# Gate products and convolution taps placed between the heads of the first attention

## What is computed

```python
h = rmsnorm(x, norm1_g)
z = h @ w_in + b_in
glu_val, glu_gate, q, k, v, g_conv, g_attn = split(z)
u = glu_val * sigmoid(glu_gate)                        # 1024 channels
y = depthwise_causal_conv(u, 31 taps) + conv_b
conv_out = silu(layernorm(y) * ln_g + ln_b) @ w_conv_out
q, k = rope(q), rope(k)                                # 16 query heads, 2 key heads
attn_out = sink_attention(q, k, v, window=128) @ w_attn_o
merged = sigmoid(g_conv) * conv_out + sigmoid(g_attn) * attn_out
x = x + merged @ w_out
```

## Time and profile before

| what | value |
|---|---|
| median of 3 runs | 1798.57 us |
| profiled execution, its own time | 1801.52 us |
| its span on the core | 1799.5 us |
| PE busy | 84% |
| DVE, ACT busy | 54%, 32% |
| granted clock of TensorE, mean | 0.95 |
| first layer up to the start of `wout` | 303.16 us of the span |

### The profile page before, as it was taken

How to read it: one execution, slowest core, us unless ns; L and a number is a source line. 1 busy time by engine, 2 the same in 40 slices (tenths; PEclk the granted TensorE clock), 3 DMA queues, 4 the chain that set the end, 5 groups by cost and what they waited for, 6 DMA issues and landing times.

```text
span 1799.5 us, 18415 instructions
## 1 busy us (share of the span) xinstructions
...
## 2 busy tenths in 40 slices
...
GB/s 256 198 214 152 1 47 141 126 408 386 389 421 420 419 420 416 411 420 419 408 409 420 398 48 173 53 94 140 130 179 176 177 111 153 63 125 188 188 187 47
DMA packets 52023, 428.69 MB, mean 238 GB/s; under 512 B 6880, under 2 KB 7032, under 8 KB 9824
## 3 DMA queue, kind: packets, MB, share of 16 engines
...
## 4 chain that ended last, share of the span: by engine, by line
PE 63%; DMA 19%; DVE 10%; ACT 5%; issue 2%; POOL 0%; DVEq 0%; SPq 0%; ACTq 0%; POOLq 0%
PE psum L595 21%; DMA pool<-uv,experts 17%; PE psum L813 10%; PE psum L686 9%; PE psum L687 9%; PE psum L688 9%; DVE pool L1473 3%; PE psum L628 2%; PE psum L644 2%; DMA ring<-stream 1%; DVE w_lo L1263 1%; ACT L1097 1%; ACT diag L1107 1%; ACT xn L904 1%; DVE hT L1198 1%
## 5 line engine op out<-in xcount | busy, mean ns | idle before, releaser
L813 PE MATMUL psum<-pool,diag 128*128 128x512 f32 x1024 | 489.1, 628 | 151.7 <-ACT diag L1107 141.9
L813 PEld LDWEIGHTS psum<-pool,diag 128*128 128x128 f32 x1024 | 195.4, 199 | 441.3 <-ACT diag L1107 223.0
L1473 DVE CUSTOM_DVE_ANT_0 pool<-pool,xn 128x1024 f32<-128x1024 f32 x256 | 313.8, 1226 | 216.5 <-DMA pool<-uv,experts 215.2
L552 POOL DMA_INDIRECT pool<-uv,experts x256 | 273.6, 1069 | 714.7 <-PE psum L813 371.7
L1263 DVE TENSOR_TENSOR w_lo<-ring,w_hi 128x2048 fp32r<-128x2048 f32 x86 | 196.8, 2292 | 218.2 <-ACT w_hi L961 218.2
L961 ACT ACTIVATE w_hi<-ring 128x2048 fp32r<-128x2048 f32 x86 | 164.3, 1914 | 326.4 <-PE psum L688 326.4
L686 PE MATMUL psum<-h_hi,w_hi 128*128 128x256 f32 x704 | 201.6, 286 | 22.4 <-DVE h_lo L1274 22.4
L687 PE MATMUL psum<-h_lo,w_hi 128*128 128x256 f32 x704 | 201.1, 286 | 0.0
L688 PE MATMUL psum<-h_hi,w_lo 128*128 128x256 f32 x704 | 201.1, 286 | 0.0
L595 PE MATMUL psum<-hT,ring 128*128 128x256 f32 x768 | 171.2, 385 | 5.4 <-DMA ring<-stream 2.8
L595 PEld LDWEIGHTS psum<-hT,ring 128*128 128x128 f32 x768 | 148.2, 193 | 28.8 <-issue 5.1
...
## 6 DMA issues: line engine op xcount, KB each, us to landing
...
pool<-uv,experts POOLq DMA_INDIRECT x256, 12.6
...
```

What stands on the lines that cost most here:

```text
L552: gp.indirect_dma_start(out=gath[:, n % NROWS, :], out_offset=None, in_=uv, in_offset=bass.IndirectOffsetOnAxis(ap=experts[:, n:n + 1], ax ...
L813: last = nc.tensor.matmul(psum[:, RB + half, :], diag[:, n % NDIAG, :], gath[:, n % NROWS, D + 512 * half:D + 512 * half + 512], start=k = ...
L1473: ins = V.tensor_tensor_reduce(out=row_u, in0=row_u, in1=xn[:, n // SLOTS, :], scale=1.0, scalar=0.0, op0=ALU.mult, op1=ALU.add, accum_out ...
```

## The change

- The gate products are made tile by tile (`GATES`, 16 of them). Six run before q and k are transposed, one after that, eight between heads of attention (after heads 0, 1, 3, 5, 7, 9, 11 and 13) and the last behind the first transposes of the attention's output. ACT no longer takes their sigmoid but copies them raw; two blocks of eight sigmoids come later (`gate_sigmoids`).
- The taps are counted through by `conv_taps(n)`: 27, 27, 27 and 67 behind the four GLU results, then the rotation, then 7 in each head of attention, 3 behind the mask and 4 behind the maximum, until all 248 are done (14 heads with 7, one with 2, one with none).
- q and k are rotated behind tap 148 instead of tap 186 (and no longer wait for the two stores, whose sources move out of `att`, to `pool` and `tab`).
- The layer norm moves behind attention: `mean` stands between the two pairs of output transposes, `var` behind the first quarter of `attno`; `attno` comes before `convout`, also in the stream of weights.
- The merge of the two branches is made in four pieces, each behind a quarter of `convout`, and `wout` waits for a piece at a time.

The diff, without the moved scratch tables, the new semaphore, the functions that only gather the transposes of the output, and the removed lines of `conv_pair`:

```diff
@@ -77,7 +77,7 @@
...
-    out += [(("convout", i), 4096) for i in range(2)] + [(("attno", i), 4096) for i in range(2)]
+    out += [(("attno", i), 4096) for i in range(2)] + [(("convout", i), 4096) for i in range(2)]
@@ -98,6 +98,27 @@
...
+GATES = [("gate", n // 4, n % 4) for n in range(16)]
+GATES_FIRST = 6
+GATE_AFTER_HEAD = {0: 7, 1: 8, 3: 9, 5: 10, 7: 11, 9: 12, 11: 13, 13: 14}
+GATE_LAST = 15
+CONV_TAPS = KD * TAPS
+TAPS_AFTER_GLU = (27, 27, 27, 67)
+TAPS_IN_HEAD = 7
+def att1_fills():
+    out = [("att1", "S", 0), ("att1", "S", 1)]
+    for h in range(QH):
+        out.append(("att1", "T", h))
+        if h + 2 < QH:
+            out.append(("att1", "S", h + 2))
+        if h in GATE_AFTER_HEAD:
+            out.append(GATES[GATE_AFTER_HEAD[h]])
+    out += [("att1", "OT", 0, t) for t in range(NT)] + [GATES[GATE_LAST], ("mean",)]
+    return out + [("att1", "OT", 1, t) for t in range(NT)]
@@ -130,10 +151,11 @@
...
-    out += fm_fills("gate", 4)
-    out += [("q1T", t, half) for t in range(NT) for half in range(2)] + [("k1T",), ("mean",), ("var",)]
-    out += attention_fills("att1", QH)
-    out += fm_fills("convout", 2) + fm_fills("attno", 2) + tm_fills("wout", 2)
+    out += GATES[:GATES_FIRST]
+    out += [("q1T", t, half) for t in range(NT) for half in range(2)] + [("k1T",), GATES[GATES_FIRST]]
+    out += att1_fills()
+    out += [("attno", 0, 0), ("var",), ("attno", 0, 1), ("attno", 1, 0), ("attno", 1, 1)]
+    out += fm_fills("convout", 2) + tm_fills("wout", 2)
@@ -158,6 +180,8 @@
...
+for i in range(4):
+    LAST_USE["gate", i] = ("gate", i, 3)
@@ -637,7 +663,21 @@
...
-            def attention(a):
+            def gate(n):
+                name, i, m = GATES[n]
+                w = wait_chunk(pe, (name, i))[:, 0:4096].rearrange("p (k n) -> p k n", k=KD)
+                dst = begin(GATES[n])
+                accumulate(dst[:, 0:S], [(w[:, k, P * m:P * m + P], hT[:, k, :]) for k in range(KD)]
+                           ).then_inc(bank_filled, 1)
+            def attention(a, gate_after={}):
@@ -669,12 +709,11 @@
...
+                    if h in gate_after:
+                        gate(gate_after[h])
...
+                if a.heads == HEADS2:
+                    turn_outputs(a, 0)
@@ -751,31 +790,54 @@
...
-            feature_major("gate", 4)
+            for n in range(GATES_FIRST):
+                gate(n)
...
-            pe.wait_ge(conv_ready, 4)
-            accumulate(begin(("mean",))[:, 0:S], [(ones, y[:, k, :]) for k in range(KD)]).then_inc(bank_filled, 1)
-            pe.wait_ge(ysq_ready, 1)
-            accumulate(begin(("var",))[:, 0:S], [(ones, ysq[:, k, :]) for k in range(KD)]).then_inc(bank_filled, 1)
+            gate(GATES_FIRST)
...
-            attention(att1)
+            attention(att1, GATE_AFTER_HEAD)
+            turn_outputs(att1, 0)
+            gate(GATE_LAST)
+            pe.wait_ge(conv_ready, 4)
+            accumulate(begin(("mean",))[:, 0:S], [(ones, y[:, k, :]) for k in range(KD)]).then_inc(bank_filled, 1)
+            turn_outputs(att1, 1)
+            wait_turned(att1)
+            def feature_major_pair(name, i, pair, act):
+                w = wait_chunk(pe, (name, i))[:, 0:4096].rearrange("p (k n) -> p k n", k=KD)
+                dst = begin((name, i, pair))
+                for j in range(2):
+                    c = P * (2 * pair + j)
+                    last = accumulate(dst[:, S * j:S * j + S], [(w[:, k, c:c + P], act[:, k, :]) for k in range(KD)])
+                last.then_inc(bank_filled, 1)
+            feature_major_pair("attno", 0, 0, oT)
+            pe.wait_ge(ysq_ready, 1)
+            accumulate(begin(("var",))[:, 0:S], [(ones, ysq[:, k, :]) for k in range(KD)]).then_inc(bank_filled, 1)
+            feature_major_pair("attno", 0, 1, oT)
+            feature_major_pair("attno", 1, 0, oT)
+            feature_major_pair("attno", 1, 1, oT)
...
-            wait_turned(att1)
-            feature_major("attno", 2, oT)
-            pe.wait_ge(merged_ready, 1)
-            token_major_chunks("wout", 2, hT)
+            for i in range(2):
+                w = wait_chunk(pe, ("wout", i))[:, 0:4096].rearrange("p (k n) -> p k n", k=KD)
+                for t in range(NT):
+                    dst = begin(("wout", i, t))
+                    for k in range(KD):
+                        if k % 2 == 0 and i == 0 and t == 0:
+                            pe.wait_ge(merged_ready, k // 2 + 1)
+                        last = nc.tensor.matmul(dst, hT[:, k, tile128(t)], w[:, k, :], start=(k == 0), stop=(k == KD - 1))
+                    last.then_inc(bank_filled, 1)
@@ -918,7 +980,27 @@
...
-            def attention(a):
+            def gate_copy(n):
+                m = n % KD
+                if n == KD:
+                    act.wait_ge(rpb_stored, 16 * RPB_ROWS)
+                empty(GATES[n], (sgc if n < KD else sga)[:, m, :], lambda b: b[:, 0:S])
+            def gate_sigmoids(g, first):
+                for n in range(first, first + KD):
+                    wait_emptied(act, GATES[n])
+                    nc.scalar.activation(g[:, n % KD, :], g[:, n % KD, :], ACT.Sigmoid, bias=par_("b_gate")[:, n:n + 1]
+                                         ).then_inc(gate_ready, 1)
+            def attention(a, gate_after={}):
@@ -1039,15 +1120,8 @@
...
-            for i in range(4):
-                for pair in range(2):
-                    b = wait_filled(act, ("gate", i, pair))
-                    for j in range(2):
-                        m = 4 * i + 2 * pair + j
-                        dst = (sgc if m < KD else sga)[:, m % KD, :]
-                        last = nc.scalar.activation(dst, b[:, S * j:S * j + S], ACT.Sigmoid,
-                                                    bias=par_("b_gate")[:, m:m + 1])
-                    last.then_inc(emptied_sem(("gate", i, pair)), 1)
+            for n in range(GATES_FIRST):
+                gate_copy(n)
@@ -1056,17 +1130,23 @@
...
+            gate_copy(GATES_FIRST)
+            attention(att1, GATE_AFTER_HEAD)
+            outputs_turned(att1, 0)
+            gate_copy(GATE_LAST)
+            outputs_turned(att1, 1)
+            gate_sigmoids(sga, KD)
...
-            nc.scalar.activation(sc_sb[:, 0, 0:S], b[:, 0:S], ACT.Sqrt, bias=eps,
+            nc.scalar.activation(deviation, b[:, 0:S], ACT.Sqrt, bias=eps,
...
-            attention(att1)
+            gate_sigmoids(sgc, 0)
@@ -1235,6 +1315,7 @@
...
+                        conv_taps(taps_in_head // 2)
@@ -1245,7 +1326,9 @@
...
-                        link(ins)
+                        n_max = mark(ins)
+                        conv_taps(taps_in_head - taps_in_head // 2)
+                        after(n_max)
@@ -1322,29 +1405,31 @@
...
+            taps_done = [0]
+            def conv_taps(count):
+                for _ in range(min(count, CONV_TAPS - taps_done[0])):
+                    pair, at = divmod(taps_done[0], 2 * TAPS)
+                    w, m = at // 2, 2 * pair + at % 2
+                    taps_done[0] += 1
+                    src, tap = u[:, m, w:w + S], conv_w[:, m, w:w + 1]
+                    if w == 0:
+                        mark(V.tensor_scalar(y[:, m, :], src, tap, par_("conv_b")[:, m:m + 1], ALU.mult, ALU.add))
+                    elif at == 2 * TAPS - 1:
+                        after(steps[0] - 1)
+                        V.scalar_tensor_tensor(y[:, m, :], src, tap, y[:, m, :], ALU.mult, ALU.add
+                                               ).then_inc(conv_ready, 1)
+                    else:
+                        after(steps[0] - 1)
+                        mark(V.scalar_tensor_tensor(y[:, m, :], src, tap, y[:, m, :], ALU.mult, ALU.add))
@@ -1354,18 +1439,16 @@
...
-                if i:
-                    conv_pair(i - 1)
...
+                conv_taps(TAPS_AFTER_GLU[i])
...
+            V.tensor_scalar(nsink, row_("sinks"), -1.0, None, ALU.mult)
...
-            dve.wait_ge(t5_stored, 16)
-            dve.wait_ge(rpb_stored, 16 * RPB_ROWS)
@@ -1381,32 +1464,34 @@
...
-            conv_pair(3)
+            attention(att1, TAPS_IN_HEAD)
+            conv_taps(CONV_TAPS)
+            def gated(name, g, first, i, pair):
+                b = wait_filled(dve, (name, i, pair))
+                m = 4 * i + 2 * pair
+                dve.wait_ge(gate_ready, first + m + 2)
+                d = g[:, m:m + 2, :].rearrange("p a b -> p (a b)")
+                V.tensor_tensor(d, d, b, ALU.mult).then_inc(emptied_sem((name, i, pair)), 1)
...
+            gated("attno", sga, 0, 0, 0)
...
-            dev = sc_sb[:, 0, 0:S]
-            link(V.reciprocal(dev, dev))
-            V.tensor_tensor(y, y, dev.unsqueeze(1).to_broadcast([P, KD, S]), ALU.mult).then_inc(ynorm_ready, 1)
-            link(V.tensor_scalar(nsink, row_("sinks"), -1.0, None, ALU.mult))
-            dve.wait_ge(ynorm_ready, 1)
-            attention(att1)
-            for name, g in (("convout", sgc), ("attno", sga)):
-                for i in range(2):
```

(24 more changed lines are left out.)

59 lines of the change are left out of this document (25 added, 34 removed).

## The result

The changed kernel took 1788.23 us (median of 9 runs, 1785.44 to 1794.89). The kernel before, in runs on the same chip, took 1800.8 us (median of 9, 1795.11 to 1802.48). The ratio of the means is 0.9941, 95% interval 0.9926 to 0.9955: 10.6 us faster, somewhere between 8 and 13 (the medians differ by 12.6). The forecast was 1789.2 us.

What follows compares the result with a forecast made beforehand. PE's idle waits and slow work behind them were taken as the bound. `wout` 7.9 us earlier plus 1.5 for its slow start gave 9.4: 1801.52 to 1792.1, less 2.95 for the median, 1789.2 us; range 1785.5 to 1796.

Steps and rivals of the forecast that it cites:

- Up to the first scores: Gate products to first scores: gate tiles start at 113.89, rotation done 123.5, DVE idles some 19 us, scores near 142.
- The head: In attention: a head with 7 taps takes DVE 4.52 us, 1.74 its own part and 2.78 the taps.
- below, nothing in the rows goes under 0.397: Lower bound on the price in us of a tap among other DVE instructions in attention.
- Rival 1: In attention: taps among other DVE instructions run at full length, 8.0 us more, time 1797.2; chance 0.10.
- DVE sets the pace: In attention: DVE needs 4.52 us a head against 3.9 of PE, so PE has short waits.
- The two waits: In attention: PE waits 5.1 us before T of head 0 and 7.3 before head 9's, restarting at low clock.
- The layer norm: Behind attention, lying under the products: PE waits only 0.3 us for the square; `wout` starts at 295.3 against 303.16.
- The rule on table loads: On ACT: the skill budgets about 2.66 us per table switch, making the square 1.4 us later, time 1790.6.
- The merge: Before `wout`: the wait of 3.21 us goes, and with it the slow start of `wout`, 1.5 us saved.
- Behind `wout`: From `wout` to the end: nothing changes; gaps differing by more than 1 us would show the forecast wrong.
- Rival 3: Behind the first layer: experts wait for gathers, scratch tables and ring could bind; gain given back, about 1798; chance 0.06.
- Rival 2: In attention: PE falls to 1.2 GHz and stays there, 43 us more, 1832; chance 0.06.

Runs made afterwards that it cites:

- e10: The changed kernel run once more, unaltered: 1789.26 us.
- e3: Changed kernel with all seven taps of a head behind its minimum, none between scores, maximum and minimum: 1782.66 us.
- e9: Changed kernel with forty taps moved between the rotation and the first scores, four instead of seven left in a head: 1787.22 us.
- e4: Changed kernel with DVE dividing the first eight heads behind the maximum of head 9 instead of head 8: 1782.52 us.
- e7: Changed kernel with both all taps of a head behind its minimum and the division behind head 9: 1776.26 us.
- e6: Changed kernel with the merge's sum made in one piece and `wout` waiting for all of it: 1794.11 us.
- e1: Changed kernel with fourteen gate tiles ahead of the transposes instead of six and none between heads, taps staying between the heads: 1807.32 us.

## Why the prediction was right, and where it was not

The forecast median was 1789.2 us, the measured one 1788.23; the forecast gain 9.4 us, the measured one 10.6. The profiled pair, however, differs by 12.9 us at the start of `wout`, where the forecast had 7.9. The sums of the prediction come out when they are redone, but for the lower end of the range: 1789.2 less 2 and 1.4 is 1785.8, not 1785.5. Point by point:

- **Up to the first scores.** Gate tiles at 113.89, measured 113.82. Rotation done at 123.5, measured 123.62. DVE idle some 19 us, measured 17.72. First scores at 142.1, measured 140.28: the slow start of the six tiles was missing in this execution, and was there in e10. 1.8 us of the 5.0.
- **The head.** This term was mis-sized: 4.52 us of DVE for a head with 7 taps, measured 4.16. I took the tap right (0.393 to 0.395 by the starts, 0.397 forecast) and the head's own part wrong: 1.74, where 1.40 are left when taps stand in between. Of the 0.36 us, e3 shows 0.26 as the time that a dependent instruction waits for the one before it (twice 0.12, and 0.02 in the rest), and 0.10 as my counting a last instruction to its end. The sentence "below, nothing in the rows goes under 0.397" bounded the tap and forgot the instructions beside it, which the interleaving makes cheaper. Rival 1, that it makes them dearer, had the sign wrong.
- **What that was worth.** Thirteen heads by 0.36 are 4.7 us, but attention ended only 2.5 us earlier (first scores at DVE to the last V: 82.8 forecast, 80.3 measured), because PE came level: DVE waited 0.58, 1.39, 2.35 and 0.49 us for scores, where the forecast had twice 1.1. e9 supports that: with 40 taps fewer in the heads, 3.7 us are gained of a possible 15.9. "DVE sets the pace" was no more than half true at 4.16. At the forecast 4.52 nothing was run; at 4.42 (e3) DVE no longer waits for scores.
- **The two waits.** 5.1 and 7.3 us forecast, 4.61 and 6.80 measured, each with T at 1.11 or 1.12 us behind. Their mechanism was right: e4 moved the division and the second fell to 0.54. The forecast took them as given; e3, e4 and e7 show that they and the slow work behind them held up to 8.6 us that could be had.
- **The layer norm.** Under the products, as forecast, with no wait before `var` where 0.3 was forecast: a sigmoid takes 0.41 us, not the 0.50 of a silu. From the last V to `wout` 68.65 us against 69.4. The rule on table loads (the Trainium skill, ScalarE: Activation LUTs, What ACT_TABLE_LOAD costs) would have had a drain besides; the load 0.02 us behind the copy (230.05 + 1.08) and the sigmoid 0.02 us behind the load show none, and 0.93 us of slack would have hidden most of it.
- **The merge.** Its wait and the slow start of `wout` are gone, 3.2 and 1.5 us forecast; putting them back cost 3.46 and 1.48 (e6).
- **Behind `wout`.** Gaps were to be the same within 1 us. That stretch is 1.3 us longer than before, so by its own sign the prediction was wrong here; but among all kernels it is 1466.9 to 1470.1 with nothing changed in it, and 1 us was too fine a sign. The one profile of the kernel before lies near the lower end and the thirteen others at 1468.7 on average, so a loss of a microsecond or two is not excluded. Rival 3, by which the whole gain is lost, falls.
- **Rival 2, the clock.** It stayed at 0.94 in attention. e1 shows how near the danger is: with PE busy 47.74 of 75.48 us, waits of 1.3 to 2.2 us before eight of the heads and the same two long ones, the clock averaged 0.82, and some heads ran their scores in 1.91 us instead of 1.03. The rule of the Trainium skill (TensorE: Matmul & The Clock Gate, A second HAM failure mode: psum-queue depth-cycling), which names short idles between matmul groups as a cause of a clock that swings, agrees with e1 in kind. The gate tiles in those gaps are what e1 took out, and with them the clock was 0.94.

The three errors, 1.8 at the start, 2.5 in attention and 0.7 behind it, all point the same way and make the 5.0 us at `wout`; the first of them is chance. That the median was hit within 1 us is partly luck. The forecast took its 9.4 us from a median of 1798.57 over three runs; from the 1800.8 of nine runs it would have said 1791.4, which is 3.2 us above the measured one. And runs of one kernel scatter over 9 us. The pair of profiles is 14.6 us apart at the end of `wout`, the means of the runs 10.6 at the end of the kernel; 1.8 of that difference is the missing slow start and 1.3 the longer rest, and no run here settles the other 0.9.
